# One tap of each convolution moved from VectorE to ScalarE in the delta stage of a decoder layer, with wider taps and two fills moved

## The reference

```python
proj = x @ w_in
qkv = jax.nn.silu(causal_depthwise_conv(qkv, conv_qkv))      # 4 taps, the "short" convolution
q, k = l2norm(q), l2norm(k)
o = gated_delta_rule(q, k, v, g, beta)                       # chunks of 64 tokens, 8 heads of 128
u = glu[..., :CONF_CH] * jax.nn.sigmoid(glu[..., CONF_CH:])
u = causal_depthwise_conv(u, dw_w) + dw_b                    # 31 taps, the "long" convolution
```

## Time and profile before

| | us |
|---|---|
| three runs, median (lowest to highest) | 2616.98 (2609.07 to 2618.28) |
| the profiled execution | 2616.05 |
| its span | 2614.5 |
| TensorE busy (share of the span) | 2399.3 (92%) |
| VectorE busy | 1762.1 (67%) |
| ScalarE busy | 1333.6 (51%) |
| GpSimd busy | 685.8 (26%) |

### The profile page before, as it was taken

The page is one execution under the profiler, slowest core; times in us unless marked ns, Lnnn a source line. Parts: engine busy times, 40 slices in busy tenths (PEclk is TensorE's granted clock), DMA queues, the critical chain, the costliest instruction groups (busy, mean ns, idle before and its releaser), DMA issues. The chain is left out here.

```text
span 2614.5 us, 40683 instructions
## 1 busy us (share of the span) xinstructions
PE 2399.3 (92%) x11739; PEld 1953.8 (75%) x11740; DVE 1762.1 (67%) x2231; ACT 1333.6 (51%) x1735; POOL 685.8 (26%) x674
## 2 busy tenths in 40 slices
PE   7989999999999899957999886899999998999995
PEld 6858777877777788846787675688888887888782
DVE  3337888788788866636754485577767786677645
ACT  3244565456456544424421132577767776667640
POOL 2002111112211111113101212544444443444330
PEclk9989999999999999978999998899999999999997
DMA  4434543332332354344665234889989999999935
GB/s 116 74 45 69 66 49 63 85 64 58 73 66 49 66 95 108 81 154 134 185 206 185 90 88 168 268 279 326 305 275 311 318 324 346 279 286 292 329 77 215
DMA packets 244142, 435.92 MB, mean 167 GB/s; under 512 B 25096, under 2 KB 149000, under 8 KB 244046
## 3 DMA queue, kind: packets, MB, share of 16 engines
q1 hardware_dynamic: 211198, 350.70, 46.0%
q0 software_dynamic: 32848, 83.96, 12.4%
HBM read 370.88 MB, written 97.71 MB: 179 GB/s over the span
## 5 line engine op out<-in xcount | busy, mean ns | idle before, releaser
L59 PE MATMUL dn_pj<-x_hi,dn_hi 128*128 128x512 f32 x1024 | 432.6, 422 | 1.8 <-PEq L84 1.8
L61 PE MATMUL dn_pj<-x_hi,dn_lo 128*128 128x512 f32 x1024 | 405.9, 396 | 0.0
L60 PE MATMUL dn_pj<-x_lo,dn_hi 128*128 128x512 f32 x1024 | 403.2, 394 | 0.0
L1058 DVE SCALAR_TENSOR_TENSOR uc_half<-u_in,par,uc_half 128x512 f32<-128x512 f32 x480 | 379.9, 791 | 13.1
L59 PE MATMUL gu_ps<-e_hi,xg_hi 128*128 (+1 forms) x752 | 311.2, 414 | 0.0
L2535 DVE TENSOR_TENSOR e_lo<-e_raw,e_hi (+1 forms) x128 | 292.4, 2286 | 21.3 <-ACT e_hi L2474 21.0
L61 PE MATMUL gu_ps<-e_hi,xg_lo 128*128 (+1 forms) x752 | 295.4, 393 | 0.0
L60 PE MATMUL gu_ps<-e_lo,xg_hi 128*128 (+1 forms) x752 | 294.6, 392 | 0.0
L2474 ACT ACTIVATE e_hi<-e_raw (+1 forms) x128 | 245.1, 1917 | 44.8 <-PEq L84 35.4
L61 PEld LDWEIGHTS dn_pj<-x_hi,dn_lo 128*128 128x128 f32 x1024 | 194.6, 190 | 44.7
L60 PEld LDWEIGHTS dn_pj<-x_lo,dn_hi 128*128 128x128 f32 x1024 | 196.1, 192 | 33.2 <-issue 1.0
(11 more groups left out here) (392 smaller groups left out, 4993.4 us busy)
## 6 DMA issues: line engine op xcount, KB each, us to landing
e_raw<-in_w_gate_e_dram SPq DMA_DIRECT2D x128, 512.0 KB, 5.5
e_raw<-in_w_up_e_dram SPq DMA_DIRECT2D x128, 512.0 KB, 7.9
e_raw<-in_w_down_e_dram SPq DMA_DIRECT2D x128, 512.0 KB, 7.8
dn_raw<-in_w_in_dram SPq DMA_DIRECT2D x64, 512.0 KB, 7.8
gate_rows<-qkv_next SPq DMA_DIRECT2D x16, 512.0 KB, 3.1
br_raw<-in_w_oa_dram SPq DMA_DIRECT2D x16, 512.0 KB, 4.4
br_gate<-gate_rows SPq DMA_DIRECT2D x32, 256.0 KB, 4.3
br_raw<-in_w_ob_dram SPq DMA_DIRECT2D x16, 512.0 KB, 3.9
```

The source lines that it names most:

```text
L59: nc.tensor.matmul(out, w_hi, x_hi, start=first, stop=False)
L60: nc.tensor.matmul(out, w_hi, x_lo, start=False, stop=False)
L61: return nc.tensor.matmul(out, w_lo, x_hi, start=False, stop=last)
L1058: ins = stt(out=uc[:], in0=u_in[:, t:t + HALF], scalar=w, in1=uc[:], op0=ALU.mult, op1=ALU.add)
```

## The change

All of it is in `delta_net`.

- `tile_move` for q, k and v keeps the copy to `rp[j]` and adds a second activation from the same PSUM tile: a copy scaled by the weight of the last tap (which is not shifted), written to `nxt`. Only this second one releases the PSUM bank. Two waits move from VectorE's `conv` to ScalarE ahead of it.
- `conv` has three taps left, each one instruction 1024 wide, and each adds to what ScalarE wrote. A tile has 3 instructions in place of 8, and each now waits for the one directly before.
- The long convolution's first tap with its bias is now an Identity activation on ScalarE, with the two waits that it had. It stands behind `glu_move` or `gate_move` and ahead of the copy L897.
- On TensorE, for p = 0, the 2 fills (3 in the last group) that stood behind the transposes of v now stand ahead of the wait for `silu_done`.
- On TensorE, one fill moves to level 6, behind L727 and ahead of L738's wait: from level 4 where there is a next group, from level 5 in the last group.

```diff
-            CONV_TILE = 1 + 2 * TAPS_S
+            STEPS = TAPS_S - 1
...
                     if p == 0:
+                        f(2 if more else 3)
                         pe.wait_ge(silu_done, g * 6 + 6)
...
-                    f(2 if more else 3)
+                    if p > 0:
+                        f(2 if more else 3)
...
-                        if l <= 4:
+                        if l <= 3:
                             f(2)
-                        elif l == 5:
+                        elif l == 4:
                             f(1 if more else 2)
+                        else:
+                            f(1)
...
-                        after(act, conv_sem, conv_no(G, p, j) * (2 * TAPS_S) - 2 * TAPS_S)
-                        A(rp[j][:, PAD:PAD + S], ps, ACT.Copy).then_inc(pj_moved, 1)
+                        after(act, conv_sem, conv_no(G, p, j) * STEPS - STEPS)
+                        A(rp[j][:, PAD:PAD + S], ps, ACT.Copy)
+                        if p == 1 and j == 0:
+                            after(act, cur_ready, G * 2)
+                        if p == 3:
+                            after(act, silu_done, G * 6)
+                        A(nxt[:, KIND[p], j, :], ps, ACT.Copy,
+                          scale=self.par[:, G * GH + j, R_SC + STEPS * 3 + KIND[p]:R_SC + STEPS * 3 + KIND[p] + 1]
+                          ).then_inc(pj_moved, 1)
...
+                    act.wait_ge(u_loaded, q * 16 + 16)
+                    act.wait_ge(uc_stored, q * 16 + 16)
+                    c = pair_of(g, p)
+                    A(uc[:], u_in[:, 0:HALF], ACT.Identity, scale=self.par[:, c, R_DW:R_DW + 1],
+                      bias=self.par[:, c, R_DWB:R_DWB + 1]).then_inc(taps_done, 1)
                     act.wait_ge(xt_t, q * 7 + 1)
...
-                        for hf in range(2):
-                            acc = nxt[:, KIND[p], j, hf * HALF:(hf + 1) * HALF]
-                            src = rp[j][:, hf * HALF + t:hf * HALF + t + HALF]
-                            if t == 0:
-                                ins = v.tensor_scalar(acc, src, w, None, ALU.mult)
-                            else:
-                                dve.wait_ge(conv_sem, base + 2 * t + hf - 1)
-                                ins = stt(out=acc, in0=src, scalar=w, in1=acc, op0=ALU.mult, op1=ALU.add)
-                            ins.then_inc(conv_sem, 1)
+                        acc = nxt[:, KIND[p], j, :]
+                        if t:
+                            dve.wait_ge(conv_sem, base + t)
+                        stt(out=acc, in0=rp[j][:, t:t + S], scalar=w, in1=acc, op0=ALU.mult, op1=ALU.add
+                            ).then_inc(conv_sem, 1)
...
-                tap_numbers = iter(range(TAPS_L))
+                tap_numbers = iter(range(1, TAPS_L))
...
-                    taps(2)
+                    taps(1)
...
-                            conv(G, p, 0, range(2, TAPS_S))
+                            conv(G, p, 0, range(2, STEPS))
...
-                        conv(G, p, 1, range(1, TAPS_S))
+                        conv(G, p, 1, range(1, STEPS))
```

More of the change, by code:

```diff
@@ L831, in tile_silu @@
                     c = conv_no(G, p, j)
-                    act.wait_ge(conv_sem, (c + 1) * 2 * TAPS_S)
+                    act.wait_ge(conv_sem, (c + 1) * STEPS)
                     if p == 3:
@@ L974, in lo, with conv @@
                     tt(r["lo"][j][:], r["raw"][j][:], r["hi"][j][:].bitcast(F32), ALU.subtract).then_inc(r["w_ready"], 1)
-                def conv(G, p, j, part=range(TAPS_S)):
+                def conv(G, p, j, part=range(STEPS)):
                     if p == 0:
                         return
-                    base = conv_no(G, p, j) * 2 * TAPS_S
+                    base = conv_no(G, p, j) * STEPS
                     if 0 in part:
                         dve.wait_ge(pj_moved, tile_no(G, p, j) + 1)
[L983 to L987, removed]
                     for t in part:
                         w = self.par[:, bass.ds(G * GH + j, 1), R_SC + t * 3 + KIND[p]]
-                        for hf in range(2):
-                            acc = nxt[:, KIND[p], j, hf * HALF:(hf + 1) * HALF]
-                            src = rp[j][:, hf * HALF + t:hf * HALF + t + HALF]
-                            if t == 0:
-                                ins = v.tensor_scalar(acc, src, w, None, ALU.mult)
-                            else:
-                                dve.wait_ge(conv_sem, base + 2 * t + hf - 1)
-                                ins = stt(out=acc, in0=src, scalar=w, in1=acc, op0=ALU.mult, op1=ALU.add)
-                            ins.then_inc(conv_sem, 1)
+                        acc = nxt[:, KIND[p], j, :]
[3 more added lines that the diff above has]
+                            ).then_inc(conv_sem, 1)
                 def glu_product(G, p):
@@ L1049, in taps @@
                             w = self.par[:, bass.ds(g * 2 + p // 2, 1), R_DW + t]
[L1050 to L1060, removed]
+                            dve.wait_ge(taps_done, 1 + q * TAPS_L + t)
+                            stt(out=uc[:], in0=u_in[:, t:t + HALF], scalar=w, in1=uc[:],
+                                op0=ALU.mult, op1=ALU.add).then_inc(taps_done, 1)
                     if p == 0:
```

## The result

The changed kernel takes 2619.78 us (median of 12 runs, 2616.74 to 2624.27) where the kernel before, run beside it on the same chips, takes 2613.61 us (12 runs, 2609.01 to 2618.32). The ratio is 1.0024, with an interval of 1.0016 to 1.0033: 6.2 us slower, a small loss that is clear of the noise. The forecast was 8.1 us slower.

What follows compares the result with a forecast made beforehand. TensorE's work plus its waits was taken to bound the kernel; terms of 2.0 + 2.9 - 8.0 + 1.8 + 4.8 + 6.1 - 3.1 + 0 + 1.6 = +8.1 us on 2616.05 gave 2624.1 us, range 2610 to 2636.

Steps and rivals of the forecast that it cites:

- Costs of the pieces: Estimated times of moved instructions: scaled copy 1.03 us plus 0.09 for the pointer, Identity tap 0.8, 1024-wide VectorE tap 1.28.
- Term 1: Prologue: the new copy stands ahead of q's and k's norms on ScalarE, at two places: +2.0 us.
- Term 2: First pair: fills ahead of v's transposes leave VectorE's L1080 to L1084 uncovered, so L691 is late: +2.9 us.
- Term 3: The three other group starts: fills run in the wait for v, L691 comes 2.7 us earlier each: -8.0 us.
- a clock that falls all the same: Fallback for the three later group starts: if the clock still drops there, the gain is -3.6 us, not -8.0.
- Terms 4 and 6: L738 delayed by copies ahead of `hi`: three pairs 1 at +0.6 us each (+1.8), three pairs 3 at +2.05 (+6.1).
- One sign: Sign of being right: L738's wait for L1107 in pairs 2 and 3 still 1.8 to 2.6 us.
- Term 5: Three pairs 2: copies delay L643 at level 3 (+0.6 us) and `hi` at level 5 (+1.0): +4.8 us together.
- Term 7: Moved fill covers L738's wait in four pairs 0 and the last group's pairs 1 to 3: -3.1 us.
- Term 8: Identity tap ahead of L897 fits ScalarE's idle time, u's DMA having landed: 0 us; +6.4 if a table load were needed.
- Term 9: Clock drops after TensorE idle times of 2 us and more: three of ten, one more than before: +1.6 us.

Runs made afterwards that it cites:

- the control: The kernel before with one empty line more and the same instructions, against the kernel before: 2611.30 us against 2611.10, ratio 0.9996.

## Why the prediction was right

The sign, the size (8.1 us against 6.2 us, and 9.05 us in this stage's trace) and the range held, and so did the mechanism: the copy ahead of `hi` and `norm` costs what it takes where TensorE waits behind it, and VectorE's saving does not pay for it. That the total came so close is in part luck. In the trace the prologue is 2.0 us and the group starts with their pairs 0 are 2.8 us above the forecast, the pairs 2 are 1.8 us and the clock drops elsewhere 1.6 us under it. Point by point:

*Costs of the pieces.* The 1024-wide tap takes 1.28 us alone, as estimated, the scaled copy 1.11 us (estimated 1.12), the Identity tap 0.80 us (0.8):

```profile
640.80 1.28 DVE L1004 SCALAR_TENSOR_TENSOR qkv_next<-pre_conv,par,qkv_next 128x1024 f32<-128x1024 f32 x1
L1004 DVE SCALAR_TENSOR_TENSOR qkv_next<-pre_conv,par,qkv_next 128x1024 f32<-128x1024 f32 x66 | 89.8, 1360 | 1.1
L813 ACT ACTIVATE qkv_next<-dn_pj,par 128x1024 f32<-128x1024 f32 x22 | 24.4, 1109 | 0.0
L910 ACT ACTIVATE uc_half<-u_in,par 128x512 f32<-128x512 f32 x16 | 12.8, 803 | 1.6 <-DMA conv_rows<-uc_half 1.6
```

The mean of the taps is 1.36 us, since nine of the 66 take 1.65 or 2.3 us. All nine run beside a GpSimd instruction; six others do too and take 1.28, so the cause is not shown.

*Term 1, prologue: right, with 2.0 us of clock on top.* The copy stands ahead of `norm` and L643 waits exactly 1.01 us longer (4.30 against 3.29 us in the earlier trace rows), twice. But TensorE arrives 4.0 us later at the first pair. The other 2.0 us are clock, for which the term had nothing: the two low stretches of the prologue are 13.7 us long each in this trace and 10.2 in the trace of before. Most of that is chance. In the control, with the instructions of before, they are 6.8 us each. In the trace of the kernel whose first pair was left as it was, with the changed kernel's prologue, they are 10.2 us, and TensorE arrives at the first pair 1.3 us late, not 4.0. The low stretches of after, in windows that lie within them:

```profile
134.80:148.20 13.40, 10.03 (x16) 5.07 (x17) 5.28 (x6) 6.68 (x8) 0.00 (x0) 0.50 0.28 39
182.60:196.00 13.40, 10.18 (x16) 5.14 (x17) 5.28 (x6) 6.67 (x8) 0.38 (x1) 0.50 0.61 99
```

*Term 2, first pair: right.* 2.67 us of idle time ahead of L693, forecast 2.9.

*Term 3, group starts: mechanism right, the clock part wrong in two of three.* TensorE at the second group's start:

```profile
439.55 0.65 PE L684 MATMUL dn_d<-ident,qkv_cur 128*128 128x128 f32 x4 [0.28 <-ACT qkv_cur L847]
442.18 2.07 PE L661 MATMUL dn_d<-o_sq,ones 128*128 128x512 f32 x2 [1.98 <-DVE v_beta L1081]
444.05 1.06 PE L693 MATMUL dn_c<-ident,inv 128*128 128x128 f32 x4
...
442.00:445.20 3.20, 3.02 (x7) 1.88 (x8) 3.20 (x6) 0.06 (x1) 0.72 (x1) 0.50 0.02 5
```

The wait for v, 3.39 us in the earlier trace rows and 2.97 at this group's start, became 0.28, and 1.98 us of idle time stand where the fills stood, as worked out. The last row is a window: the clock is low in it. I had counted the 1.5 us of clock as won. In the last group's start the clock stayed up, and there the gain was 2.95 us. Together with the +0.2 to L738 in place of -0.4, where part of the low stretch lies, the two starts missed the forecast by 1.6 and 1.4 us, about the price of one drop each. The prediction's own figure for a clock that falls all the same, 1.2 us a start, fits these two.

*Terms 4 and 6, pairs 1 and 3: right.* +0.6 and +2.0 us a pair. Turning the order of ScalarE's two instructions gave back what was put down to it in pair 3 (1.0 us) and 0.4 us more than that in pair 1. One sign did not hold: L738's wait in pairs 3 is 1.41 us, under the 1.8 to 2.6 given, since the fill's move put 1.22 us of the wait at level 5.

*Term 5, pair 2: too high by 0.6 us.* L643 at level 3 waits 1.68 us where it waited 0.68, as forecast:

```profile
571.37 1.10 PE L643 MATMUL dn_d<-norm_sq,ones 128*128 128x512 f32 x2 [1.68 <-ACT norm_sq L860]
```

But TensorE and ScalarE came to that place 0.43 us earlier, and 0.54 of the 0.57 us that were left of the delay went at level 4, where TensorE had waited for VectorE. I had taken 0.15 and 0.25 us for these. The part that was mis-sized is what VectorE's shorter queue gives back: about 1.0 us, not 0.4. It is not the short convolution's alone: with the Identity tap alone TensorE is ahead by the same 0.43 us there.

*Term 7, the covering fill: right in the last group*, 0.56 us a pair.

*Term 8, the Identity tap: right that it costs nothing in the changed kernel, incomplete in its reason.* The term looked at u's DMA alone, and the store of the previous result, which the tap also waits for, has not always landed. Taken alone the tap gained 0.5 us in each pair 2 in the trace and 6.7 us by the times, for which the forecast had no term.

*Term 9, the clock: the count was right, by luck.* Behind the group starts and the long waits there were five drops before and three after, and three after is what I had counted. But only three L738 waits were as long as 2 us, not six, and of the three drops one stands behind these and two stand at group starts, where the waits are 1.98 us. The control's trace has five too, one of them at another place than in the trace of before. A single trace draws its drops anew, so a difference of one says nothing; only the mean over runs does.

## What to carry to other kernels

Work moved to a less busy engine is paid for where it stands in that engine's queue, not by its load: ask which instruction is next in the queue and who waits for that. Here 1.0 us of copy ahead of a conversion cost 1.0 us each time, and behind it nothing. Ahead of a norm it cost 1.0 us in pair 3, and in pair 2 it was given back one level later, where TensorE had waited for VectorE anyway. A fill placed at the largest wait pays only as long as nothing was hidden at its old place: the first instance of a loop, where the wait does not exist, has to be looked at by itself. And when one engine waits at the end of a chain on another, first look for work in that queue that can go behind the awaited instruction: moving one tap behind it took 0.8 us off the wait in each pair 2, and it cost no other engine anything.

## What the runs showed of the hardware

The granted clock fell after idle times of TensorE that were well under the 3.4 us of the later group starts, and not after others as long. In the trace of before it fell after one L738 wait of 2.0 us and one of 2.6, and stayed up after seven of 2.0 to 2.6. In the changed kernel it fell in two of three starts with 1.98 us idle, and in its first pair it stayed up after 2.67 us. Two traces with the same instructions (before and control) have 10.2 and 6.8 us of low clock at each of the same two places of the prologue. An edit can therefore be worth more than the waits that it takes away: 2.4 us taken from three waits of 2.6 us went with 6.8 us less in the median and with a higher mean clock. It need not be these waits that draw the drops, since the Identity tap alone, which shortened no wait at L738, went with 6.7 us less.
